# Retention of a hybrid decoder step computed in chunks of 128 tokens with a carried state

## The reference, cut to what matters

```python
scores = einsum('bthk,bshk->bhts', q, k) * decay[None]          # decay = gamma^(t-s) for s <= t
o = einsum('bhts,bshv->bthv', scores, v) + einsum('bthk,bhkv->bthv', q, s0) * q_dec   # gamma^(t+1)
s_new = exp(c * log_gamma) * s0 + einsum('bshk,bshv->bhkv', k * k_dec, v)             # gamma^(c-1-s)
```

## Time and profile before

| | |
|---|---|
| runs | 1766.88, 1769.54, 1772.71 us (median 1769.54) |
| span of the profiled execution | 1765.4 us |
| mean granted PE clock | 0.930 of 2.4 GHz |
| PE busy | 1585.4 us, 90% of the span, 12187 instructions |
| DVE, ACT, POOL busy | 930.3, 657.9, 154.2 us |
| HBM over the span | 78 GB/s |

### The profile page before, as it was taken

How to read it: one execution, slowest core, us unless ns; L and a number is a source line. 1 busy time by engine, 2 the same in 40 slices (tenths; PEclk the granted TensorE clock), 3 DMA queues, 4 the chain that set the end, 5 groups by cost and what they waited for, 6 DMA issues and landing times.

```text
span 1765.4 us, 31743 instructions
## 1 busy us (share of the span) xinstructions
PE 1585.4 (90%) x12187; PEld 1263.6 (72%) x12187; DVE 930.3 (53%) x1493; ACT 657.9 (37%) x936; POOL 154.2 (9%) x126
## 2 busy tenths in 40 slices
PE   4699999998879999999957999999896999999994
PEld 3577777776658888878745777777674888887883
DVE  5766744443575555533266767444366555553334
ACT  3635423232263433422154544233235443333223
POOL 3111110000020000000030111100002000000002
PEclk8789889998989999999978989999987999999997
DMA  5121231220312233223321222222121323322321
GB/s 185 51 62 51 73 109 62 84 73 26 96 50 94 95 95 95 73 79 90 97 66 48 73 73 73 76 85 73 50 74 47 96 95 95 95 80 71 98 65 51
DMA packets 175036, 137.86 MB, mean 78 GB/s; under 512 B 5064, under 2 KB 169192, under 8 KB 174776
## 3 DMA queue, kind: packets, MB, share of 16 engines
q1 hardware_dynamic: 168192, 113.46, 21.1%
q0 software_dynamic: 5408, 18.60, 3.1%
q10 hardware_dynamic: 1372, 4.95, 0.8%
HBM read 124.91 MB, written 12.07 MB: 78 GB/s over the span
## 4 chain that ended last, share of the span: by engine, by line
PE 76%; DVE 10%; ACT 6%; issue 4%; DVEq 3%; ACTq 1%; DMA 1%; SPq 0%
PE ACC L506 60%; PE SCR L619 2%; PE SCR L536 2%; PE OT L627 2%; ACT WH L825 1%; PE SCR L657 1%; DVE X L1189 1%; PE OT L679 1%; DVE Z L1220 1%; PE OT L595 1%; DVE Fb L1202 1%; DVE WL L1149 1%; DVEq L1259 1%; PE SCR L722 1%; PE OT L594 1%
## 5 line engine op out<-in xcount | busy, mean ns | idle before, releaser
L506 PE MATMUL ACC<-XH,WH 128*128 128x280 f16 x2432 | 503.7, 290 | 74.7 <-DVE XL L1192 43.1
L506 PE MATMUL ACC<-XL,WH 128*128 128x280 f16 x2432 | 502.6, 289 | 0.0
L506 PE MATMUL ACC<-XH,WL 128*128 128x280 f16 x2432 | 502.2, 289 | 0.0
L506 PEld LDWEIGHTS ACC<-XH,WH 128*128 128x128 f16 x2432 | 237.4, 101 | 158.7 <-DVE XL L1192 45.9
L1149 DVE SCALAR_TENSOR_TENSOR WL<-stage,WH 128x2048 f16<-128x2048 f32 (+1 forms) x116 | 245.9, 2120 | 180.8 <-ACT WH L825 169.1
L506 PEld LDWEIGHTS ACC<-XL,WH 128*128 128x128 f16 x2432 | 243.4, 100 | 58.8
L506 PEld LDWEIGHTS ACC<-XH,WL 128*128 128x128 f16 x2432 | 243.5, 100 | 58.4
L825 ACT ACTIVATE WH<-stage 128x2048 f16<-128x2048 f32 (+1 forms) x116 | 204.8, 1765 | 103.0 <-PE ACC L506 85.7
L506 PE MATMUL ACC<-shared,WH 128*128 128x280 f16 x1408 | 225.4, 283 | 0.2
L506 PEld LDWEIGHTS ACC<-shared,WH 128*128 128x128 f16 x1408 | 137.6, 98 | 30.7 <-issue 0.8
L506 PE MATMUL ACC<-shared,WL 128*128 128x280 f16 x704 | 141.3, 283 | 0.0
(11 more groups left out here) (241 smaller groups left out, 1870.7 us busy)
## 6 DMA issues: line engine op xcount, KB each, us to landing
stage<-in_w_in_dram SPq DMA_DIRECT2D x64, 512.0 KB, 4.8
stage<-in_w_a_dram SPq DMA_DIRECT2D x44, 512.0 KB, 4.2
stage<-in_w_b_dram SPq DMA_DIRECT2D x44, 512.0 KB, 4.6
stage<-in_w_down_dram SPq DMA_DIRECT2D x32, 384.0 KB, 3.1
stage<-in_w_down_dram SPq DMA_DIRECT2D x32, 320.0 KB, 3.4
out_dram<-shared POOLq DMA_DIRECT2D x16, 512.0 KB, 3.4
stage<-in_w_o_dram SPq DMA_DIRECT2D x16, 512.0 KB, 3.9
shared<-in_state_hgrn_dram POOLq DMA_DIRECT2D x8, 512.0 KB, 5.8
```

The lines of the kernel that those rows point to most:

```text
L506: last = mm(ACC[:, acc, h, 0:HALF], lhs, x[:, xk + k, h * HALF:(h + 1) * HALF], start=begin, stop=end)
```

## The change

Scores are computed within blocks of 128 tokens only (four full ones and 16 tokens). Queries carry gamma^(t+1) (512 columns at once, in place, and the last 48), the scores are masked with a causal table and scaled by gamma^-(s+1) per key, so the decay tables go. Each block's key-value product goes to `SC` as a running state: DVE copies the first and adds each next to the decayed one before; a fifth step makes the final state, which POOL stores from there. An output block is the state before it times its queries plus its own masked scores times its values. The keys of all full blocks share one decay, so ACT copies them in one instruction; its copy of the final state goes. Steps move to other slots. The diff, cut to its core:

```diff
-RT_COLS = [TP - P * i for i in range(TT5)]
-RT_OFF = [sum(RT_COLS[:i]) for i in range(TT5)]
+RT_W = [P] * 4 + [TAIL]
+RT_SPLIT = 2 * P
+QDEC = P + TAIL + TS
...
-                        ("keep", T), ("masks", len(LEVELS) * C), ("mask32", TS), ("seq", DEC_BATCH), ("decay", HEADS * TP),
-                        ("mask_rt", HEADS * TS), ("q_dec", HEADS * TS), ("k_dec", TT5 * HEADS), ("k_dec_s", HEADS),
-                        ("gamma4", HEADS)]:
+                        ("keep", T), ("masks", len(LEVELS) * C), ("mask32", TS), ("seq", DEC_BATCH), ("causal", P),
+                        ("q_dec", HEADS * QDEC), ("k_inv", HEADS), ("k_inv_s", HEADS), ("k_dec", HEADS), ("k_dec_t", HEADS),
+                        ("k_dec_s", HEADS), ("gamma", 3 * HEADS)]:
...
-        PTR = part(RT_OFF[-1] + TAIL)
+        PTR = part(TP)
...
-                    head_states(l, p, 1, s0_rt_v, sn_rt_v, fin_rt_v, RSB[:, :])
+                    head_states(l, p, 1, s0_rt_v, sn_rt_v, fin_rt_v, SC[:, (TT5 - 1) * P:TT5 * P])
...
                 def scores(n):
-                    bank = 1 - n % 2
+                    bank = 1 - n
                     job(scr, bank)
-                    for i, t0, t1, o in RT_JOBS[n]:
-                        rows_ = P if i < 4 else TAIL
-                        last = mm(SCR[0:rows_, bank, o:o + t1 - t0], KE[:, i * P:i * P + rows_], QD[:, t0:t1], start=True, stop=True)
-                    if n == len(RT_JOBS) - 1:
+                    for i in ((0, 1, 2, 3), (4,))[n]:
+                        o = i * P if n == 0 else 0
+                        last = mm(SCR[0:RT_W[i], bank, o:o + RT_W[i]], KE[:, i * P:i * P + RT_W[i]], QD[:, i * P:i * P + RT_W[i]],
+                                  start=True, stop=True)
+                    if n == 1:
                         last = mm(SCR[0:TS, bank, TAIL:TAIL + TS], KE[:, TP:T], QD[:, TP:T], start=True, stop=True)
                     last.then_inc(scr_full, 1)
 
-                def final_state():
-                    pe.wait_ge(tok_ready, hh + 1)
-                    job(scr, 0)
-                    for i in range(TT5):
-                        r = P if i < 4 else TAIL
-                        last = mm(SCR[:, 0, 0:P], KTOK[0:r, i * P:(i + 1) * P], VTOK[0:r, i * P:(i + 1) * P], start=(i == 0), stop=(i == 4))
+                def state_steps(n):
+                    if n == 0:
+                        pe.wait_ge(tok_ready, hh + 1)
+                    bank = 1 - n
+                    job(scr, bank)
+                    for i in ((0, 1, 2, 3), (4,))[n]:
+                        o = i * P if n == 0 else 0
+                        last = mm(SCR[:, bank, o:o + P], KTOK[0:RT_W[i], i * P:(i + 1) * P], VTOK[0:RT_W[i], i * P:(i + 1) * P],
+                                  start=True, stop=True)
                     last.then_inc(scr_full, 1)
 
-                def output(h):
-                    if h == 0:
+                def output(i):
+                    if i == 0:
                         pe.wait_ge(pts_ready, hh + 1)
+                        pe.wait_ge(rt_states_ready, l * HEADS + p + 1)
                         pe.wait_ge(s0_in, 16 * (hh + 1))
                         pe.wait_ge(ot_read, 1 + l * OT_LAYER + 1 + HEADS + 2 * p)
-                    a, b = ((0, SPLIT), (SPLIT, TP))[h]
-                    tiles = [i for i in range(TT5) if i * P < b]
-                    for i in tiles:
-                        r, t0 = (P if i < 4 else TAIL), max(a, i * P)
-                        mm(OT[:, h, t0 - a:b - a], VTOK[0:r, i * P:(i + 1) * P],
-                           PTR[0:r, RT_OFF[i] + t0 - i * P:RT_OFF[i] + b - i * P], start=(i == 0), stop=(i == tiles[-1]),
-                           skip_group_check=True)
-                    if h == 1:
-                        sample_output(QS).then_inc(ot_full, 1)
+                    t, w, h = i * P, RT_W[i], int(i >= 2)
+                    o = OT[:, h, t - h * RT_SPLIT:t - h * RT_SPLIT + w]
+                    if i:
+                        mm(o, SC[:, (i - 1) * P:i * P], QD[:, t:t + w], start=True, stop=False)
+                    mm(o, VTOK[0:w, i * P:(i + 1) * P], PTR[0:w, t:t + w], start=(i == 0), stop=True)
+                    if i == TT5 - 1:
+                        sample_output(QD, RT_SPLIT).then_inc(ot_full, 1)
...
-                steps += [(RT_SLOTS[1][n], lambda n=n: scores(n)) for n in range(len(RT_JOBS))]
-                steps += [(RT_SLOTS[2][0], final_state)]
+                steps += [(RT_SLOTS[1][n], lambda n=n: scores(n)) for n in range(2)]
+                steps += [(RT_SLOTS[2][n], lambda n=n: state_steps(n)) for n in range(2)]
                 steps += [(RT_SLOTS[3][n], lambda n=n: sample_steps(hh, scr, n, 1 - n)) for n in range(2)]
-                steps += [(RT_SLOTS[4][h], lambda h=h: output(h)) for h in range(2)]
+                steps += [(RT_SLOTS[4][i], lambda i=i: output(i)) for i in range(TT5)]
...
-                for i in range(4):
-                    last = f(KTOK[:, i * P:(i + 1) * P], SCR[:, 0, i * P:(i + 1) * P], ACT.Copy, scale=tab[:, ds(k_at + i * HEADS + p, 1)])
-                last.then_inc(scr_read[0], 1)
...
+                f(KTOK[:, 0:4 * P], SCR[:, 0, :], ACT.Copy, scale=tab[:, ds(k_at + p, 1)]).then_inc(scr_read[0], 1)
...
-            def rt_b(l, p, scr):
-                hh = l * 2 * HEADS + HEADS + p
-                full, _ = scr.job(0)
-                act.wait_ge(fin_stored, 16 + 16 * hh)
-                act.wait_ge(scr_full, full)
-                f(RSB[:, :], SCR[:, 0, 0:P], ACT.Copy).then_inc(scr_read[0], 1)
-                act.drain().then_inc(fin_ready, 1)
+
+            def rt_b(l, p):
                 act.wait_ge(ot_full, l * OT_LAYER + 2 + HEADS + 2 * p)
-                f(SQ[:, 0:SPLIT], OT[:, 0, 0:SPLIT], ACT.Copy)
-                f(SQ[:, SPLIT:T], OT[:, 1, 0:REST], ACT.Copy).then_inc(ot_read, 1)
+                f(SQ[:, 0:RT_SPLIT], OT[:, 0, 0:RT_SPLIT], ACT.Copy)
+                f(SQ[:, RT_SPLIT:T], OT[:, 1, 0:T - RT_SPLIT], ACT.Copy).then_inc(ot_read, 1)
...
-                tt(QS[:, TP:T], QD[:, TP:T], tab[:, ds(cols["q_dec"][0] + p * TS, TS)], ALU.mult)
+                q_at = cols["q_dec"][0] + p * QDEC
+                blocks = QD[:, 0:4 * P].rearrange("p (i t) -> p i t", t=P)
+                tt(blocks, blocks, tab[:, ds(q_at, P)].unsqueeze(1).to_broadcast([P, 4, P]), ALU.mult)
+                tt(QD[:, 4 * P:T], QD[:, 4 * P:T], tab[:, ds(q_at + P, TAIL + TS)], ALU.mult)
...
-                bank = 1
-                for job in RT_JOBS:
-                    full, _ = scr.job(bank)
-                    dve.wait_ge(scr_full, full)
-                    for i, t0, t1, o in job:
-                        r = P if i < 4 else TAIL
-                        u, w = t0 - i * P, t1 - t0
-                        last = tt(PTR[0:r, RT_OFF[i] + u:RT_OFF[i] + u + w], SCR[0:r, bank, o:o + w],
-                                  tab[0:r, ds(decay_at + p * TP + u, w)], ALU.mult)
-                    if job is RT_JOBS[-1]:
-                        last = tt(PTSS[:, :], SCR[0:TS, bank, TAIL:TAIL + TS], tab[0:TS, ds(cols["mask_rt"][0] + p * TS, TS)], ALU.mult)
-                    last.then_inc(scr_read[bank], 1)
-                    bank = 1 - bank
+                g_at, inv_at = cols["gamma"][0], cols["k_inv"][0]
+                full, _ = scr.job(1)
+                dve.wait_ge(scr_full, full)
+                stt(out=PTR[:, 0:4 * P].rearrange("p (i t) -> p i t", t=P), in0=SCR[:, 1, :].rearrange("p (i t) -> p i t", t=P),
+                    scalar=tab[:, ds(inv_at + p, 1)], in1=causal.unsqueeze(1).to_broadcast([P, 4, P]),
+                    op0=ALU.mult, op1=ALU.mult).then_inc(scr_read[1], 1)
+                full, _ = scr.job(0)
+                dve.wait_ge(scr_full, full)
+                stt(out=PTR[0:TAIL, 4 * P:TP], in0=SCR[0:TAIL, 0, 0:TAIL], scalar=tab[0:TAIL, ds(inv_at + p, 1)],
+                    in1=causal[0:TAIL, 0:TAIL], op0=ALU.mult, op1=ALU.mult)
+                stt(out=PTSS[:, :], in0=SCR[0:TS, 0, TAIL:TAIL + TS], scalar=tab[0:TS, ds(cols["k_inv_s"][0] + p, 1)],
+                    in1=mask32[0:TS, :], op0=ALU.mult, op1=ALU.mult).then_inc(scr_read[0], 1)
                 dve.drain().then_inc(pts_ready, 1)
+
+                dve.wait_ge(fin_stored, 16 + 16 * hh)
+                full, _ = scr.job(1)
+                dve.wait_ge(scr_full, full)
+                nc.vector.tensor_copy(SC[:, 0:P], SCR[:, 1, 0:P])
+                for i in range(1, 4):
+                    dve.drain()
+                    last = stt(out=SC[:, i * P:(i + 1) * P], in0=SC[:, (i - 1) * P:i * P], scalar=tab[:, ds(g_at + p, 1)],
+                               in1=SCR[:, 1, i * P:(i + 1) * P], op0=ALU.mult, op1=ALU.add)
+                last.then_inc(scr_read[1], 1)
+                dve.drain().then_inc(rt_states_ready, 1)
+                full, _ = scr.job(0)
+                dve.wait_ge(scr_full, full)
```

(46 more changed lines are left out.)

3 lines of the change are left out of this document (removed).

## The result

Eight executions of each kernel give 1773.45 us after (1772.42 to 1775.11) and 1769.11 us before (1766.88 to 1772.71): ratio 1.0023, 95% interval 1.0014 to 1.0032, so 4.3 us slower by the medians, where 1765 us was forecast. The traced execution has a span of 1772.7 us, 7.3 more than the one before. That is more than the medians differ by: the trace of before is of one of its faster executions (experiment 11 has one with a span of 1769.6 us).

What follows compares the result with a forecast made beforehand. Retention heads were taken as a loop of one PE part and three set by ACT and DVE, hiding most saved PE work. 1.4 - 0.8 - 2.0 - 0.6 - 2.8 = -4.8 us gave 1765 us, range 1754 to 1777.

Steps and rivals of the forecast that it cites:

- the clock rival: "Slower through the clock": waits at slots 16 and 24 bring 1.2 GHz, 1.8 us per stretch; 1776 us, up to 1780; chance 0.22.
- the sum takes no net change beyond the 2.0 above: Clock: a 1.85 us wait may cost 1.8 us or nothing; only the half-clock stretch's -2.0 us was counted.
- the six retention stretches: Between successive `rest_transposes`: three give -0.8 us, the 42.4 us one -2.0, the two of 41.2 us -0.6.
- the moved slots: `rest_transposes` go from slot 6 to 7, 0.72 us later before each layer's first head: +1.4 us in two layers.
- the last heads: Last retention head of each layer, inside the output projection: -1.4 us each, -2.8 in two layers.
- 7.16 us: From the end of slot 11's states through DVE's state chain and `split_lo(1)` to slot 16; PE waits 1.1 us.
- The first slots: PE from `rest_transposes` through slots 7 to 10, scores and states: 5.4 us.
- the outputs: PE's outputs, products of slots 16 and 17, and sample output: 5.65 us.
- outputs' end to slot 24: From the sample output's end to slot 24, set by ACT and DVE: unchanged 7.71 us, PE's wait growing to about 2.5.
- slot 24 to the variance: The longer query decay lies on this path: 4.00 us becomes 4.64, while PE needs 3.58 and waits.
- 18 matmuls: PE work of a retention head after the change, at most 128 columns each: 4.4 us for 6.75, saving 2.3 us.
- The saved PE work shows: Rival: PE sets the pace and up to 2.3 us a head comes out: 1752 us; chance 0.22, wholly or in part.

Runs made afterwards that it cites:

- experiment 11: Kernel before, unchanged, run again for the trace of a second execution: 1771.71 us.
- experiment 3: Kernel before with both weight halves made early in the retention heads (low on DVE, next head's high on ACT): 1773.47 us, ratio 1.0007.
- experiment 4: Kernel after with one idle DVE operation of 560 columns in each layer's second normalisation: 1767.63 us, ratio 0.9991.
- experiment 13: Kernel before with three idle DVE operations (560, 560 and 100 columns) in each layer's second normalisation: 1778.93 us, ratio 1.006.
- experiment 12: Kernel before with three idle DVE operations (560, 560 and 400 columns) in each layer's second normalisation: 1774.14 us, ratio 1.0045.
- experiment 8: Kernel after, unchanged, run again beside the kernel before, twelve executions: 1772.39 us, ratio 1.0007.
- experiment 5: Kernel before with PE's wait in the HGRN heads filled (sample products later, ACT's query read earlier): 1748.56 us, ratio 0.9873.
- experiment 6: Kernel after with PE's wait in the HGRN heads filled (sample products later, ACT's query read earlier): 1744.74 us, ratio 0.9857.
- experiment 2: Kernel after with both weight halves made early in the retention heads (low on DVE, next head's high on ACT): 1746.26 us, ratio 0.9862.

## Why the prediction was wrong

The measured 1773.45 us lies inside the stated range of 1754 to 1777 us, but the change went the other way, and the range reached that far for the clock rival alone, which put the loss into the retention stretches.

**What failed.** The step that failed is "the sum takes no net change beyond the 2.0 above", in the paragraph on the clock. It looked for the clock's part in the six retention stretches alone. The HGRN stage, in which nothing was changed, was taken as fixed, and it holds nearly all of the difference between the traces: HGRN stages 0.87 + 7.60 us (1.44 of it the moved slots), retention stages -1.65 - 0.31, the rest +0.79; together 7.3. Experiments 3, 4 and 13 show that the chunked form is neither enough for the long stage nor needed for it: with a pause upstream, which moves its start by under 3 us, it was short in the kernel after and long in the kernel before. That the start of the stage decides is likely, but not shown: the longer pause of experiment 12 left it short, and the kernel after as it is has faster executions too (three of twelve in experiment 8). Experiments 5 and 6 show that without the long heads the change is not slower. In the changed code itself the sum is 1.44 for the slots + 1.86 in six stretches - 3.86 in the last heads = -0.6 us, where -4.8 was forecast.

**The mis-sized term.** "7.16 us" from the end of slot 11's states to slot 16 measured 7.77 (289.31 to 297.08). The copy and three steps took 1.66 for 1.54, the gap to the next step 0.32 for 0.16, and from DVE's last read to PE's first output it was 0.39 for 0.06. Times six that is 3.7 of the 5.3 us by which the stretches missed (+1.86 for -3.4); the part at 1.2 GHz behind slot 24 in the two first stretches is another 1.2.

**What held.** The first slots took 5.40 us (5.40 forecast), the outputs 5.67 (5.65), outputs' end to slot 24 7.71 (7.71), slot 24 to the variance 4.63 in the second stretch (4.64), from there to the next `rest_transposes` 9.83 to 9.92 (9.85). The waits are 1.19 us at slot 16 (1.1), 2.31 at slot 24 of the first stretch (2.5) and 0.70 at `rest_transposes` (0.75). The first of them agrees by luck: PE's own work up to slot 16 was also put too low, 6.03 us for 6.58 (7.77 less the wait). PE's idle time rose by 8.9 us (span less busy; some 10 forecast). Its busy time, which was to fall by 15 or more, fell by 10.8 us in the two retention stages and only by 1.6 in all: it rose by 9.2 us in the two HGRN stages, where PE had the same work, but for the moved slots (1.4 us), and layer 2's at a lower clock. The last heads gained 1.66 and 2.20 us (1.4 each). The "18 matmuls" are 19 by the loops, beside the sample's scores (five for scores, five for states, nine for outputs); the terms of the sum count them rightly.

**The rivals.** "The saved PE work shows" is false for the kernel as changed and true in experiment 2: it needs the two moves. "Slower through the clock" had the mechanism in the wrong place: PE does run at 1.2 GHz after the wait at slot 24 of each layer's first stretch, but that costs 0.6 us there (5.25 to the variance for 4.63), not 1.8. After the 1.19 us at slot 16 the products run at full speed, 0.40 us a row, up to the next wait.

The Trainium skill, "TensorE: Matmul & The Clock Gate", Part 1 (What's actually happening), says besides that what gates the clock runs free and does not begin anew with a kernel. The traces agree as far as they go: executions of one kernel fall some 7 us apart (experiment 8: 1764.1 to 1764.9 and 1771.6 to 1774.7 us) at granted clocks of 0.927 to 0.930 and 0.924 to 0.925.
